# Sliding attention's rotated queries, the decay rows of two other mixers, two gate tiles and four orders of work in a ten-stage block on one NeuronCore

## The reference

```python
for i, mixer in enumerate((conv, fox, gdn, swa)):      # first block
    x = x + mixer(rms_norm(x, norm_w[i]))
x = rms_norm(x, final_norm_w)
h = rms_norm(x, g_mix_2)                               # second block
y_sb = stick_breaking(sb_q, sb_k, sb_v)                # 8 heads of 64
y_ml = mlstm(ml_q, ml_k, ml_v, ml_i, ml_f)             # 4 heads of 128
y_xa = cross_attention(xa_q, mem)                      # 4 heads of 128, 256 memory rows
x = x + (sum over the branches of gate * (y @ w_out)) @ w_o
x = x + (silu(u_gate) * u_val) @ w_down                # u = conv(rms_norm(x) @ w_up), width 2816
```

```python
def rope(x):                     # swa: 16 query heads of 64, 4 key heads; half = 32
    return concat(x1 * cos - x2 * sin, x2 * cos + x1 * sin)
# fox: logits[q, k] = q.k * scale + c[q] - c[k], with c = cumsum(log_sigmoid(f_logit)), one row a head
# gdn: beta = sigmoid(h @ w_beta); g = -exp(a_log) * softplus(h @ w_a + dt_bias); 8 heads, one row each
#      T = inverse of (1 + L) by chunks of 64; then a state that is updated in 4 chunks of 128 in the kernel
# mlstm: i = h @ w_i + b_i; f = log_sigmoid(h @ w_f + b_f): 4 rows each, and their running maxima m
```

## Time and profile before

| | |
|---|---|
| median of 3 runs | 2179.13 us (2178.32 to 2180.03) |
| the profiled execution's own time | 2175.7 us |
| its span | 2173.9 us |
| mean granted clock of PE | 0.991 |
| busy: PE, DVE, ACT, POOL | 2092.8, 1476.8, 553.1, 338.5 us |

### The profile page before, as it was taken

The page is one execution under the profiler, slowest core; times in us unless marked ns, Lnnn a source line. Parts: engine busy times, 40 slices in busy tenths (PEclk is TensorE's granted clock), DMA queues, the critical chain, the costliest instruction groups (busy, mean ns, idle before and its releaser), DMA issues.

```text
span 2173.9 us, 31824 instructions
## 1 busy us (share of the span) xinstructions
PE 2092.8 (96%) x12924; PEld 1630.2 (75%) x12924; DVE 1476.8 (68%) x2239; ACT 553.1 (25%) x969; POOL 338.5 (16%) x322
## 2 busy tenths in 40 slices
PE   8999999999899999899998999998999999999998
PEld 6888777777677777677777666766778888788786
DVE  6666566666767776477888677555556778858775
ACT  1001122232544444224662133432220011000000
POOL 2111111111100000011112111100112222112121
PEclk9999999999999999999999999999999999999999
DMA  4332322221211122122122221111223332232322
GB/s 167 107 97 88 97 68 78 68 68 60 80 51 63 61 65 61 40 88 78 59 69 87 70 77 58 59 40 35 63 73 102 97 107 87 88 107 81 111 78 90
DMA packets 51313, 169.62 MB, mean 78 GB/s; under 512 B 6608, under 2 KB 6736, under 8 KB 50912
## 3 DMA queue, kind: packets, MB, share of 16 engines
q1 hardware_dynamic: 48688, 162.31, 24.1%
q10 hardware_dynamic: 2480, 5.28, 0.7%
HBM read 165.43 MB, written 2.13 MB: 77 GB/s over the span
## 4 chain that ended last, share of the span: by engine, by line
PE 77%; DVE 18%; issue 2%; ACT 2%; DMA 0%; ACTq 0%; DVEq 0%; POOL 0%; SPq 0%
PE ps_lin L1689 20%; PE ps_lin L1690 19%; PE ps_lin L1691 19%; PE ps_att L1735 11%; PE ps_aux L1735 5%; DVE arena L412 5%; DVE w_lo L406 4%; DVE arena L406 2%; DVE arena L409 1%; ACT arena L1201 1%; DVE y_lo L406 1%; DVE v_tmp L406 1%; PE ps_att L1738 1%; PE ps_lin L1706 1%; DVE y_hi L449 1%
## 5 line engine op out<-in xcount | busy, mean ns | idle before, releaser
L1689 PE MATMUL ps_lin<-xw_hi,w_hi 128*128 128x512 f32 (+1 forms) x1744 | 719.5, 413 | 11.0 <-DVE w_lo L406 11.0
L1691 PE MATMUL ps_lin<-xw_hi,w_lo 128*128 128x512 f32 (+1 forms) x1744 | 683.5, 392 | 0.0
L1690 PE MATMUL ps_lin<-xw_lo,w_hi 128*128 128x512 f32 (+1 forms) x1744 | 683.3, 392 | 0.0
L388 POOL TENSOR_SCALAR w_hi<-raw 128x1024 fp32r<-128x1024 f32 (+3 forms) x314 | 334.1, 1064 | 1820.4 <-PE ps_lin L1691 1693.0
L406 DVE TENSOR_TENSOR w_lo<-raw,w_hi 128x1024 fp32r<-128x1024 f32 (+3 forms) x314 | 379.5, 1209 | 48.4 <-POOL w_hi L388 18.6
L1201 ACT ACTIVATE arena<-arena 128x512 f32<-128x512 f32 (+7 forms) x311 | 194.0, 631 | 806.6 <-DVE arena L412 371.3
L1689 PEld LDWEIGHTS ps_lin<-xw_hi,w_hi 128*128 128x128 f32 (+1 forms) x1744 | 325.6, 187 | 95.2 <-DVE w_lo L406 15.4
L1691 PEld LDWEIGHTS ps_lin<-xw_hi,w_lo 128*128 128x128 f32 (+1 forms) x1744 | 325.2, 186 | 75.0 <-issue 0.3
L1690 PEld LDWEIGHTS ps_lin<-xw_lo,w_hi 128*128 128x128 f32 (+1 forms) x1744 | 325.9, 187 | 73.2 <-issue 9.3
L406 DVE TENSOR_TENSOR arena<-ps_lin,rstd 128x512 f32<-128x512 f32 (+2 forms) x213 | 146.5, 688 | 233.7 <-PE ps_lin L1691 221.4
L1689 PE MATMUL ps_lin<-y_hi,w_hi 128*128 128x512 f32 (+1 forms) x560 | 213.4, 381 | 7.6 <-DVE y_lo L406 5.1
(11 more groups left out here) (166 smaller groups left out, 1750.7 us busy)
## 6 DMA issues: line engine op xcount, KB each, us to landing
raw<-in_w_up SPq DMA_DIRECT2D x44, 512.0 KB, 3.5
raw<-in_conv_w_in SPq DMA_DIRECT2D x32, 512.0 KB, 3.6
raw<-in_fox_w_in SPq DMA_DIRECT2D x32, 512.0 KB, 3.5
raw<-in_gdn_w_in SPq DMA_DIRECT2D x32, 512.0 KB, 3.5
raw<-in_w_gate SPq DMA_DIRECT2D x24, 512.0 KB, 3.5
raw<-in_swa_w_in SPq DMA_DIRECT2D x20, 512.0 KB, 3.5
raw<-in_w_ml SPq DMA_DIRECT2D x16, 512.0 KB, 3.5
raw<-in_w_down SPq DMA_DIRECT2D x16, 512.0 KB, 3.6
```

Source lines behind the costliest of these rows:

```text
L388: pool.tensor_scalar(w_whole(n, kc * c)[0], w_raw(n, kc * c), 1.0, 0.0, mult, add).then_inc(s("w_rounded"), 1)
L1689: pe.matmul(o, wh, hi, start=first and k == 0, stop=False)
L1690: pe.matmul(o, wh, lo, start=False, stop=False)
L1691: ins = pe.matmul(o, wl, hi, start=False, stop=last and k == kc - 1)
```

## The change

1. Swa: `swa_rotate` goes. ACT, behind its copy of the raw queries, issues four transfers inside SBUF, each 32 partitions × 2 KB, that exchange the halves (`qt`). The minus sign is in the sines. DVE multiplies `qt` (in SBUF) where it multiplied `ps_aux`.
2. Fox and mLSTM: `spread` goes. The rows are written to DRAM once, and each head's row is read back with a broadcast to 128 partitions (256 KB, issued by ACT).
3. `gdn_w_beta` and `gdn_w_a` become one tile of 40 columns, `ml_w_i` and `ml_w_f` one of 36. At the delta net's entry the rows' chain is written in another order: softplus first, Tanh beside it, the sums before beta.
4. Delta-net heads: fills moved from "A" to the levels, DVE's subtraction in halves (`weight_halves`), the scale of the previous output at level 4, its split in chunk 0.
5. Cross attention: two query tiles are evacuated ahead of the last log weights; the last stick-breaking product follows the first squares and a tile.
6. FFN: down group 1 comes after all up tiles; the last two u blocks get buffers of their own.

The diff, cut:

```diff
-    tile("gdn_w_beta", 0, ND, GDN_H, "xw2")
-    tile("gdn_w_a", 0, ND, GDN_H, "xw2")
+    tile("gdn_w_gates", 0, ND, 32 + GDN_H, "xw2")
...
-            if g and j == a:
+            if g == 1 and j == a:
                 for m in range(ND):
                     tile("w_down_2", m, KU, P, "u", k0=groups[g - 1][0], tag=("down", g - 1, m))
+    for m in range(ND):
+        tile("w_down_2", m, KU, P, "u", k0=groups[1][0], tag=("down", 1, m))
...
-        GDN_FILL = {"tok": 4, "squares": 4, "A": 4, "U0": 3}
+        GDN_FILL = {"tok": 4, "squares": 4, "A": 0, "U0": 3}
+        LEVEL_FILL = (0, 2, 2, 1, 1, 2, 1)
...
+            def weight_halves(t):
...
+                    for half in (slice(0, T), slice(T, 2 * T)):
+                        ins = tt(w_lo[:, n % SPLIT, half], raw[:, n % RAW, half], w_hi[:, n % SPLIT, half].bitcast(f32), sub)
...
                 fill(GDN_FILL["A"])
-                if h:
-                    gdn_out_scale(h - 1)
...
-                        fill(1)
+                        if l == 4 and h:
+                            gdn_out_scale(h - 1)
...
+                    fill(LEVEL_FILL[l])
...
+                    if c == 0 and 0 < h < GDN_H - 1:
+                        split(v_tmp[:], y_hi[:, h - 1, :], y_lo[:, h - 1, :], "y_ready")
...
-                        if c == 1 and h:
-                            split(v_tmp[:], y_hi[:, h - 1, :], y_lo[:, h - 1, :], "y_ready")
...
             def swa_rope(j):
 
-                dve.wait_ge(s("swa_qrot"), j + 1)
-                step(tt(F["s2"], ps_aux[:], F["sin"], mult))
+                dve.wait_ge(s("swa_qrot"), 64 * (j + 1))
+                step(tt(F["s2"], F["qt"], F["sin"], mult))
...
+                if n == SB_H - 1:
+                    dve.wait_ge(s("sb_z"), NT * SB_H)
+                    for h in range(2):
+                        evac(tile_of("w_xa", h), xa["q"][:, h, :])
...
+            def fox_row(h):
+
+                act.dma_start(F["cb"], fox_rows[h].partition_broadcast(P)).then_inc(s("fox_cb"), 16)
...
                 if h >= 0:
-                    act.wait_ge(s("fox_bc"), h + 1)
-                    activation(F["cb"], ps_aux[:], ACT.Copy).then_inc(s("fox_cb"), 1)
-                    act.wait_ge(s("fox_cb"), made("fox_cb"))
                     for i in range(NT):
...
+                    if h < FOX_H - 1:
+                        fox_row(h + 1)
...
                 activation(F["qr"], ps_lin[:, t % BANKS, :], ACT.Copy).then_inc(bank_read(t), 1)
+                act.wait_ge(bank_read(t), reads(t))
+                half = HD // 2
+                for to in range(0, P, half):
+                    src = to + half if to % HD == 0 else to - half
+                    act.dma_start(F["qt"][to:to + half, :], F["qr"][src:src + half, :]).then_inc(s("swa_qrot"), 16)
...
-                    pe.wait_ge(*aux("fox_cb", h + 1))
-                    spread(ps_aux[:], F["c"], 8, h).then_inc(s("fox_bc"), 1)
...
                 if j < ND - 1:
-                    project(ND // 2)
-                    swa_rotate(j + 1)
-                    project(ND // 2)
+                    tile()
...
-                            spread(ps_aux[:], F["nm"], 4, h).then_inc(s("ml_bc"), 1)
...
-                            spread(ps_att[:, 3, :], F["m"], 4, h).then_inc(s("ml_bcm"), 1)
...
-            tile()
-            sb_pv(SB_H // 2 - 1)
...
+            tile()
             xa_squares(0)
             tile()
+            sb_pv(SB_H // 2 - 1)
```

168 lines of the change are left out of this document (95 added, 73 removed).

## The result

The changed kernel takes 2139.88 us (median of 4 runs, 2138.89 to 2144.56) against 2178.73 of before (4 runs, 2176.14 to 2180.03): ratio 0.9827, 95% interval 0.981 to 0.9845. That is 38.9 us less; the forecast was 2124, with 55.5 less, and the range 2112 to 2138. The profiled execution took 2140.55 us, span 2138.7, clock 0.991; 35.2 less than the profiled one of before.

A forecast was written before the change was run, and what follows sets the result against it. It took TensorE (PE) as the bound, busy 96% of the span and 77% of the chain. Terms summed to −55.5 us: 2175.7 profiled to 2120.2, with 3.4 added 2123.6 median, so 2124; range 2112 to 2138.

The forecast's parts named there:

- Swa queries, 0: Sliding attention: PE loses eight rotations, but DVE waits for the transfers, so 0 per pair; −1.5 to +4 us for seven.
- Rival (b): Waits move instead of going: late swa transfers, smaller gains in delta-net heads, entry and FFN; −40.9 us, 2138; chance 0.22.
- (a): Swa: PE's share decides there too, so the eight rotations are gained; −9 us, 2115; chance 0.12.
- (c): More goes than counted: clock stays high at both entries, delta-net heads lose all waits; −61 us, 2118; chance 0.10.
- Rival (d): Swa: PE idle time in each pair drops the clock to 1.2 GHz for seven pairs; +111 us, 2235; chance 0.02.
- mLSTM heads, −7.6: mLSTM heads: spreads replaced by transfers save four times 1.91 us; −7.6, bounds −6 to −8.
- fox: Fox: eight spreads of 1.12 us leave PE, worth 1.08 each; −8.6 us, bounds 7.5 to 9.
- the delta-net entry: Delta-net entry: one gate tile less (−5.5) and 3.3 of the 4.20 wait gone; −8.8 us, bounds −5.5 to −9.7.
- cross attention: Cross attention's entry: waits of 6.8 us go, plus 2.4 from the low clock; −9.2 us, bounds −5 to −10.
- the merged gate tiles: mLSTM gates: one weight tile less, rows needed only behind later tiles; −5.5 us, bounds −4 to −5.5.
- heads: Delta-net heads: no PE work goes, only waits, chiefly L754's 9.1 us, and small gaps; −11 us, bounds −5 to −14.
- the FFN: FFN's end: wait of 5.12 and about 2 us of slow clock go, 2.4 come back in up tiles; −4.8 us.

The follow-up runs named there:

- e13: Changed kernel with VectorE evacuating swa's gate tile ahead of the rope operations: 2144.12 us, ratio 0.9847.
- e10: Changed kernel, unchanged, profiled again in another execution: 2142.58 us.
- e12: Kernel before with fox's rows by transfer alone: 2170.61 us, ratio 0.9975.
- e3: Changed kernel with two swa transfers of 64 partitions in place of four, exchanging heads instead of halves, for timing alone: 2136.91 us, ratio 0.9815.
- e14: Changed kernel with ACT copying swa's raw queries as soon as the tile is done, DVE's product with the cosines waiting for it: 2138.79 us, ratio 0.9825.
- e2: Kernel before with the swa transfers of the change alone: 2185.94 us, ratio 1.0042.
- e17: Changed kernel with mLSTM's turned values copied first and swa's four transfers issued by GpSimd instead of ACT: 2131.41 us, ratio 0.9794.
- e6: Kernel before with mLSTM's rows by transfer alone, no spreads: 2175.61 us, ratio 0.9993.
- e4: Changed kernel with ACT's copy of mLSTM's turned values moved ahead of the silu of the next head's queries: 2133.11 us, ratio 0.9801.
- e7: Kernel before with cross attention's entry in the new order alone: 2170.48 us, ratio 0.9968.
- e11: Kernel before with the delta-net heads' part alone: 2168.23 us, ratio 0.9954.

## Why the prediction was wrong

**The step that failed: "Swa queries, 0".** Its first half was right: DVE waits for the transfers about what it used to idle, PE's saving turns into PE's idle time. What failed is the landing's size, the path over ACT, and the clock, which the term put at nothing; in their place the stage got 10.9 us longer. Two of the prediction's signs of being wrong came: a period above 18 (18.03) and a granted clock under 1 in swa (0.97).
- Landing: I took 3.3 us from the end of the raw copy, bounds 2.5 to 4.5; it is 1050.63 − 1046.67 = 3.96. Four issues of 0.61 (2.45 together), of which the last begins 1.83 after the first and lands 2.0 later. My 0.36 to 0.58 per issue, from one read back and two writes, was too low. DVE's wait is 2.51 instead of 1.85, which is the pair's +0.7.
- ACT: I wrote that the turned copies come 1.5 to 2 us later, and let it pass because PE's product with the values "starts about where it did". They come 2.58 later, PE waits 1.90 for them, and e13 shows that this path alone holds 18.03.
- Where the 10.9 is. The four steady intervals have 4 × 0.7 = 2.8. The first three between scores were 13.74, 16.96 and 17.31 before and are 17.81, 16.11 and 19.93 after: +5.8. In front of the first scores it is +0.7, behind the last +1.6. I had allowed up to 4 for all, from the steady pair.
- The clock. The 13.7 us at 1.2 GHz lie in these other parts, about 10.3 from just before the first scores to the fourth and 3.4 behind the last. What such a stretch costs is seen where one falls among steady pairs (e10: 19.45 + 18.24 against 2 × 18.03, 1.6 for 3.4 us) and behind the last scores in e12 (65.72 against 64.39 in before, 1.3 for 3.4 us). By this the clock is 5 to 6.5 of the 10.9, an estimate.
- The start, for the rest. Only a pair that is full has the 1.85 of slack: PE's wait in front of the first scores is 3.12, where it was 1.58, and a new one of 2.06 stands in front of the second. In e3 and e14, with the clock whole there, the first interval is still 15.43 against 13.74. With the estimate for the clock, 1.5 to 3 us of the 10.9 are left for the start and the end.

Rival (b) had the late landing ("the transfers in swa land late") with 4 us and 0.22, and its sum, 2138, was the nearest to 2139.9. That is in part luck: it missed 11 us of loss in swa and mLSTM's heads, and gave away 7 us in the delta-net heads, the entry and the FFN that were gained. Rivals (a) and (c) are refuted: no rotation was gained, and the heads lost less than all of their waits. Rival (d), the clock in swa, was right in kind and far off in size: 13.7 us at the lower level and not seven pairs. The waits of 1.90 in the steady pairs left the clock whole in the first profile; in e10 and in e2 one such pair has a half-speed stretch (19.45, 19.50). With the transfers, the eleven profiles have 3.4 to 13.7 us at 1.2 GHz in the stage; with the product, nine profiles have none or 3.4. Which wait decides isn't shown.

The mean clock of the whole is 0.991 in both first profiles: what the change gave back at cross attention's entry and at the FFN's end, swa took.

The estimate worked out from the Trainium skill (DMA: Bandwidth & Descriptors, Anatomy of one DMA), 2.15 us for 64 KB and a loss of about 0.4 a pair, agrees with the 2.2 measured for ACT's transfers of 64 KB (the median from issue to landing) and with the 2.2 of GpSimd's own in e17. A pair lost 0.7: the issues on ACT took longer than the prediction's rows had them, and the path over ACT was as long.

**"mLSTM heads, −7.6": half of it came back.** Measured −1.9 to −3.3. The spreads are gone, 2.1 a head, and in two of the four heads the next wait on PE's path takes it: ACT's copy of the turned values is queued behind a silu that waits for DVE's convolution, 0.63 before, 2.71 after. The prediction says nothing about what would be late next. e6 shows it alone. e4 takes it away, and 1.8 of it comes back in PE's waits for the squares (3.9 us together in the changed kernel, 5.7 in e4).

**Right within the noise:** fox (−8.6; −9.6 and −7.1, e12 the stretch −9.6), the delta-net entry (−8.8; −8.6 twice: the wait 4.20 became 1.37), cross attention (−9.2; −9.8 and −9.0, e7 −9.9), the merged gate tiles (−5.5; −7.0, in which the first head's spread, and clock, are mixed). **Somewhat too large:** heads (−11; −8.4 and −5.6, e11 −8.9; L754's waits went from 9.1 to 2.4, so the mechanism is right, 2.4 of them stayed, and the gaps beside them, which I put at 0.3 and 1.4, gave less; the stretch itself moves by 2.7 between profiles) and the FFN (−4.8; −3.6 and −3.3: 1.7 came back in listed waits, the rest in smaller gaps).

The profile of before, the base of my sum, ran a stick-breaking stage without a slow stretch; the other has one. This is 3.1 us of the 20.3 between the forecast's 55.5 and the 35.2 of the first pair of profiles, and none in the second pair. Beside it stand 10.9 in swa, 4.3 in the mLSTM heads and 2.6 in the delta-net heads; the other stretches together are 0.6 better than forecast.

## What to carry to other kernels

When a product is replaced by transfers, follow both chains behind it: the one that waits for the data, and whatever is queued on the engine that issues them (here 0.61 us an issue, 2.45 in all, which cost as much as the landing). A slack that is read from the steady state isn't there in the first rounds of a loop: cost these by themselves, and look at the granted clock there: waits of 2 to 3 us stood beside its fall here. And where a saving in front of a wait is forecast, look up how long the next wait on the same engine already is: if what it waits for doesn't move, the saving goes there.

## What was not expected of the hardware

The granted clock isn't a property of the program: with the same kernel, 1394 to 1454 ran at 1.00 in one execution and at 0.94 in another, and single parts that gained 9.6 and 9.9 us in their own stretch gained 5.4 and 7.0 in all. A change of under 5 us can't be judged here by one profile, only by the stretch it touches, and by that only where the clock in it is the same before and after.

A transfer between partitions of 64 KB takes 2.2 us from issue to landing (median; the ones issued just behind a 512 KB load in e14 took 3.6 to 4.2) and one of 128 KB 3.1, and the issue keeps ACT for 0.61 each; GpSimd took 2.04 for four.
